# High parts of the split weights in three places of 1 MB, and the first expert's bias behind its tile's first row

## What is computed

```
u    = rms_norm(x);  proj = u @ w_in                    # 1024 x 4608
conv = silu(layer_norm(depthwise_conv31(a * sigmoid(g)))) @ w_conv_out
attn = block attention with ALiBi and q/k norm (8 heads) @ w_attn_out
h    = x + (sigmoid(gates) * [conv, attn] mixed) @ w_out
moe  : top 4 of 32 experts; each expert 1024 -> 2048 -> 1024 (clamped SwiGLU)
out  = h + sum of the chosen experts, weighted
```

## Time and profile before

| what | value |
|---|---|
| median of 3 runs | 1077.91 us (1076.74 to 1078.06) |
| the profiled execution | 1077.8 us, span of its instructions 1076.0 us |
| mean granted PE clock | 0.917 of full |
| PE busy | 901.7 us (84%) |
| DVE busy | 440.4 us (41%) |
| ACT busy | 253.9 us (24%) |
| DMA | 432.96 MB, mean 402 GB/s over the span |
| chain that ended last | PE 59%, DMA 31% |

### The profile page before, as it was taken

How to read it: one execution, slowest core, us unless ns; L and a number is a source line. 1 busy time by engine, 2 the same in 40 slices (tenths; PEclk the granted TensorE clock), 3 DMA queues, 4 the chain that set the end, 5 groups by cost and what they waited for, 6 DMA issues and landing times.

```text
span 1076.0 us, 18595 instructions
## 1 busy us (share of the span) xinstructions
PE 901.7 (84%) x6874; PEld 407.1 (38%) x6875; DVE 440.4 (41%) x1111; ACT 253.9 (24%) x410; POOL 5.5 (1%) x35
## 2 busy tenths in 40 slices
PE   8999999987665779699966999987996965997666
PEld 8889996322211223133311333322331311332122
DVE  6998885432222214244422344432442322343222
ACT  5578753211111101122211122220121201112111
POOL 2000000000000000000000000000000000000000
PEclk9999999997888789899977999997998988998788
DMA  9754699999999999999999999999999999999997
GB/s 329 281 191 142 264 385 416 421 431 428 434 434 434 431 430 429 432 432 434 435 429 430 432 431 435 434 430 430 429 435 431 434 434 430 429 432 432 434 421 290
DMA packets 34022, 432.96 MB, mean 402 GB/s; under 512 B 3029, under 2 KB 5489, under 8 KB 19152
## 3 DMA queue, kind: packets, MB, share of 16 engines
q1 hardware_dynamic: 33472, 431.99, 95.2%
q10 hardware_dynamic: 528, 0.66, 0.2%
HBM read 431.59 MB, written 1.05 MB: 402 GB/s over the span
## 4 chain that ended last, share of the span: by engine, by line
PE 59%; DMA 31%; another core or an unknown queue 5%; SPq 3%; DVE 1%; issue 0%; ACT 0%; DVEq 0%
PE bank L1564 23%; PE bank L1601 11%; PE bank L1255 9%; DMA down_even<-in_w_down 8%; DMA up_even<-in_w_up_gate 8%; DMA up_odd<-in_w_up_gate 8%; DMA down_odd<-in_w_down 6%; PE bank L1542 3%; PE bank L1495 3%; PE bank L1193 3%; PE bank L1474 3%; SPq L500 2%; SPq L504 1%; DMA down_odd<-in_w_in 1%; PE bank L1578 1%
## 5 line engine op out<-in xcount | busy, mean ns | idle before, releaser
L1564 PE MATMUL bank<-up_even,reg_r 128*32 128x512 f32 x1472 | 194.7, 685 | 77.0 <-DMA up_even<-in_w_up_gate 77.0
L1564 PE MATMUL bank<-up_odd,reg_r 128*32 128x512 f32 x1408 | 189.2, 693 | 70.0 <-DMA up_odd<-in_w_up_gate 70.0
L1149 DVE SCALAR_TENSOR_TENSOR ys<-bank,gslot,ys 64x512 fp32r<-64x512 f32 x90 | 67.4, 749 | 228.5 <-ACT ys L759 227.1
L759 ACT ACTIVATE ys<-bank,gslot 64x512 fp32r<-64x512 f32 x90 | 61.5, 683 | 315.4 <-PE bank L1601 314.3
L1564 PEld LDWEIGHTS bank<-up_even,reg_r 128*32 128x32 f32 x1472 | 51.0, 124 | 217.4 <-issue 131.8
L1564 PEld LDWEIGHTS bank<-up_odd,reg_r 128*32 128x32 f32 x1408 | 50.7, 125 | 205.1 <-issue 124.5
L753 ACT ACTIVATE reg_m<-reg_m 128x256 f32<-128x256 f32 x45 | 18.8, 418 | 428.5 <-DVE reg_m L1128 428.5
L1601 PE MATMUL bank<-down_odd,reg_r 128*32 128x512 f32 x704 | 85.1, 617 | 11.3 <-DMA down_odd<-in_w_down 11.3
L1601 PE MATMUL bank<-down_even,reg_r 128*32 128x512 f32 x736 | 83.7, 595 | 6.9 <-DMA down_even<-in_w_down 6.9
L1128 DVE TENSOR_SCALAR reg_m<-bank 128x256 f32<-128x256 f32 x45 | 19.1, 424 | 169.1 <-PE bank L1564 169.1
L753 ACT ACT_TABLE_LOAD x45 | 57.7, 1283 | 3.2 <-issue 2.5
(11 more groups left out here) (277 smaller groups left out, 1011.0 us busy)
## 6 DMA issues: line engine op xcount, KB each, us to landing
up_odd<-in_w_up_gate SPq DMA_DIRECT2D x29, 4096.0 KB, 46.5
up_even<-in_w_up_gate SPq DMA_DIRECT2D x28, 4096.0 KB, 39.7
down_even<-in_w_down SPq DMA_DIRECT2D x15, 4096.0 KB, 42.4
down_odd<-in_w_down SPq DMA_DIRECT2D x14, 4096.0 KB, 46.7
down_even<-in_w_in SPq DMA_DIRECT2D x16, 1024.0 KB, 5.2
up_even<-in_w_up_gate SPq DMA_DIRECT2D x5, 2048.0 KB, 13.7
up_odd<-in_w_up_gate SPq DMA_DIRECT2D x3, 2048.0 KB, 11.1
up_odd<-in_w_up_gate SPq DMA_DIRECT2D x6, 1024.0 KB, 45.4
```

What stands on the lines that cost most here:

```text
L759: nc.scalar.activation(ys[0:64, half, :], YB[r, :], ACT.Identity, scale=gslot[r, :]).then_inc(y_high, 1)
L1149: nc.vector.scalar_tensor_tensor(ys[64:P, half, :], YB[r, :], gslot[0:64, :], ys[0:64, half, :].bitcast(F32), ALU.mult, ALU.subtract).then ...
L1564: ins = mm(UP[q * SLOTS:(q + 1) * SLOTS, :], XT[:, k, :], up_columns(a, k, q), start=False, stop=(k == KD - 1), skip_group_check=True)
```

## The change

It has four parts.

1. **Three places for high parts.** `w_hi` becomes three tensors of 1 MB, rows 0, 1 and 2 of UP_EVEN. Half (i, b) uses place (2i + b - 2) modulo 3. A half's high part may now be written once PE is through with the half three before it: (i, 0) after (i-2, 1), and (i, 1) after (i-1, 0). Group 0's second half is kept as one piece in place 2.
2. **Row 3 of UP_EVEN is loaded early.** SP issues it behind rows 6 and 7, at about 23 us. Behind group 11 the order changes: nothing of UP_EVEN at the first half of group 11, row 0 at its second half, row 1 at the first half of group 12, row 2 at its end.
3. **Taps and low parts in a new order.** On ACT high part (2, 1) moves behind the two sigmoids of group 1. On DVE low part (2, 1) moves behind the first three tap rounds of the first two channel blocks, and later low parts are placed anew among the taps; the number of tap rounds ahead of head 0 stays 16.
4. **The first expert's bias.** The bias product ahead of the first gather goes; in its place are two products of zeros (`clear`). In the first expert's tiles row 0 clears the bank, and the bias is added behind it. In the first group PE waits for the first half of `u_hi` alone before it begins.

```diff
-        w_hi = [part("w_hi0", EVEN_AT, 0, 4096), part("w_hi1", EVEN_AT, 4096, 4096)]
+        w_hi = [part(f"w_hi{j}", EVEN_AT, 2048 * j, 2048) for j in range(3)]
...
+            return [w_hi[(2 * i + b - 2) % 3][:, :].rearrange("p (k n) -> p k n", k=4)] + [
+                t[:, 2048 * b:2048 * b + 2048].rearrange("p (k n) -> p k n", k=4) for t in (w_lo[place(i)], slots[place(i)])]
...
             load_up(0, 3, 0)
+            load_up_rows(0, 3, 4, 0)
...
             for b in range(2):
                 half_used(sp, OUT_W, b)
-                load_up_rows(0, 2 + b, 3 + b, 0)
+                if b == 1:
+                    load_up_rows(0, 0, 1, 0)
                 load_down(0, b, 1 + b, 0)
             half_used(sp, OUT_W + 1, 0)
-            load_up_rows(0, 0, 1, 0)
+            load_up_rows(0, 1, 2, 0)
             load_down(0, 2, 3, 0)
             used(sp, OUT_W + 1)
-            load_up_rows(0, 1, 2, 0)
+            load_up_rows(0, 2, 3, 0)
...
-                if 2 <= i < ATT_W:
-                    half_used(act, i - 2, b)
+                if i >= 2:
+                    half_used(act, *((i - 2, 1) if b == 0 else (i - 1, 0)))
...
-            for b in range(2):
-                weights_high(2, b)
+            weights_high(2, 0)
             for b in range(2):
                 (sigmoids of group 1)
+            weights_high(2, 1)
...
-            for b in range(2):
-                weights_low(2, b)
+            weights_low(2, 0)
...
-                taps(0, 5, (2 * b, 2 * b + 1))
+                taps(0, 3, (2 * b, 2 * b + 1))
+                if b == 0:
+                    weights_low(2, 1)
...
-            taps(5, 6); low(3,0); taps(6, 7); low(3,1); taps(7, 9); low(4,0); taps(9, 10); low(4,1); taps(10, 14); low(5,0); low(5,1)
+            low(3,0); taps(3, 5); low(3,1); taps(5, 7); low(4,0); taps(7, 9); low(4,1); taps(9, 10); low(5,0); taps(10, 11); low(5,1)
...
-            taps(14, 15); low(6,0); taps(15, 16); low(6,1)
+            taps(11, 13); low(6,0); taps(13, 15); low(6,1); taps(15, 16)
...
-            bias(0)
+            for j in range(2):
+                clear(j)
...
-                                 start=False, stop=(k == KD - 1), skip_group_check=True)
+                                 start=(first and k == 0), stop=(k == KD - 1), skip_group_check=True)
...
+                    if first and k == 0:
+                        bias(n, clear=False)
```

More of the change, by code:

```diff
@@ L299, in place @@
             return 1 + (i - 1) % 2 if i else 0
-        def w_whole(i):
-            return [t.rearrange("p (k n) -> p k n", k=KD) for t in (w_hi[i % 2][:, :], w_lo[place(i)][:, :], slots[place(i)])]
         def w_half(i, b):
-            return [t[:, 2048 * b:2048 * b + 2048].rearrange("p (k n) -> p k n", k=4)
-                    for t in (w_hi[i % 2], w_lo[place(i)], slots[place(i)])]
+            return [w_hi[(2 * i + b - 2) % 3][:, :].rearrange("p (k n) -> p k n", k=4)] + [
+                t[:, 2048 * b:2048 * b + 2048].rearrange("p (k n) -> p k n", k=4) for t in (w_lo[place(i)], slots[place(i)])]
+        first_low, first_whole = [t.rearrange("p (k n) -> p k n", k=KD) for t in (w_lo[0][:, :], slots[0])]
+        first_split = [w_hi[2][:, :].rearrange("p (k n) -> p k n", k=KD), first_low[:, :, 256:512], first_whole[:, :, 256:512]]
         def w_split(i, b):
-            if i == 0:
-                return [t[:, :, 256 * b:256 * b + 256] for t in w_whole(i)]
-            return w_half(i, b)
+            return first_split if i == 0 else w_half(i, b)
         def arrived(eng, i, b):
@@ L404, in load_parameters @@
                 sp.dma_start(wr[:], w_router.rearrange("(p k) n -> p k n", k=KD)).then_inc(small_in, 16)
-            first = w_whole(0)[2]
+            first = first_whole
             for c in range(4):
@@ L849, in _ @@
                 dve.wait_ge(a_ready, b + 1)
-                taps(0, 5, (2 * b, 2 * b + 1))
+                taps(0, 3, (2 * b, 2 * b + 1))
+                if b == 0:
+                    weights_low(2, 1)
             early_taps = 16
-            taps(5, 6)
             weights_low(3, 0)
-            taps(6, 7)
+            taps(3, 5)
             weights_low(3, 1)
+            taps(5, 7)
+            weights_low(4, 0)
             taps(7, 9)
-            weights_low(4, 0)
+            weights_low(4, 1)
             taps(9, 10)
[L860 to L863, removed]
+            weights_low(5, 0)
+            taps(10, 11)
+            weights_low(5, 1)
             dve.wait_ge(qk_std, 1)
@@ L875, in _ @@
                 nc.vector.tensor_tensor(v, v, f, ALU.mult).then_inc(qk_scaled, 1)
-            taps(14, 15)
+            taps(11, 13)
             weights_low(6, 0)
+            taps(13, 15)
+            weights_low(6, 1)
             taps(15, early_taps)
-            weights_low(6, 1)
             def attention_low(c):
@@ L1203, in product3_by_part @@
                     for k in range(n):
+                        if (a, b) == (0, 0) and k % 4 == 0:
+                            pe.wait_ge(u_hi_ready, k // 4 + 1)
                         if b == 1 and k % 4 == 0:
@@ L1209, in first_group_bank @@
             def first_group_bank(low):
-                w = w_whole(0)
+                w = first_split
                 u = group_use(0, 1)
                 pe.wait_ge(w_hi_ready, 1)
-                pe.wait_ge(u_hi_ready, 2)
                 claim(u)
                 for c in range(2):
-                    ins = product3_by_part(bank[u % 4][:, c * T:(c + 1) * T], lambda a, k: w[a][:, k, (2 + c) * P:(3 + c) * P],
+                    ins = product3_by_part(bank[u % 4][:, c * T:(c + 1) * T], lambda a, k: w[a][:, k, c * P:(c + 1) * P],
                                            lambda a, k: u_r[a][:, k, :], KD, low)
@@ L1221, in channel_group_bank @@
                 split(i, b)
-                w = w_whole(i)
+                w = [w_half(i, 0), w_half(i, 1)]
                 u = group_use(i, b)
@@ L1226, in channel_group_bank @@
                     ch = 2 * b + c
-                    ins = product3(bank[u % 4][:, c * T:(c + 1) * T], lambda a, k: w[a][:, k, ch * P:(ch + 1) * P],
+                    ins = product3(bank[u % 4][:, c * T:(c + 1) * T], lambda a, k: w[k // 4][a][:, k % 4, ch * P:(ch + 1) * P],
                                    lambda a, k: u_r[a][:, k, :], KD, before=before if c == 0 else None)
@@ L1237, in _ @@
                         pe.wait_ge(g0_in[k // 2], 16)
-                    ins = mm(bank[U_G % 4][:, c * T:(c + 1) * T], w_whole(0)[2][:, k, c * P:(c + 1) * P], xg[:, k, :],
+                    ins = mm(bank[U_G % 4][:, c * T:(c + 1) * T], first_whole[:, k, c * P:(c + 1) * P], xg[:, k, :],
                              start=(k == 0), stop=(k == KD - 1))
@@ L1491, in _, with bias @@
             mm(bank[U_WIDE % 4][0:E, 0:1], tri[0:E, 0:E], wide[:], start=True, stop=True).then_inc(bank_full[U_WIDE % 4], 1)
-            def bias(n):
+            def bias(n, clear=True):
                 pe.wait_ge(sel_ready, n + 1)
-                mm(UP[:], sel[:], bup[:], start=True, stop=False, skip_group_check=True)
+                mm(UP[:], sel[:], bup[:], start=clear, stop=False, skip_group_check=True)
             pe.wait_ge(counts_read, 1)
             pe.wait_ge(bup_in, 64)
-            bias(0)
+            for j in range(2):
+                clear(j)
             freed(pe, U_WIDE)
```

## The result

| | before | after |
|---|---|---|
| median | 1077.35 us (8 runs, 1076.52 to 1078.92) | 1081.53 us (8 runs, 1079.35 to 1084.28) |
| profiled execution, its span | 1077.8, 1076.0 | 1080.56, 1078.7 |

A forecast was written before the change was run, and what follows sets the result against it. The saturated DMA stream was taken to bound the kernel. The early MB's -2.44 us was given back by PE's release being 2.6 us late against 2.6 - 2.44 of remaining cover: 0.0, so 1077.8 us, range 1075.3 to 1080.0.

The forecast's parts named there:

- Where the stream is full: DMA at its end from the fifth slice on; by the windows busy at share 1.00, 430 GB/s, from 141 to 1056 us.
- DVE's waits: Before head 0, DVE newly idles 1.7 us for the transposes and 4.9 for high part (2,1); head 0 at 83.7, 5 us late.
- Up to 0.3 us later ... I take 0: Group 3's raw weights behind the early row: a delay up to 0.3 us would be hidden by late DVE; cost 0.
- PE held 1.9 us, then 0.7: PE waits for DVE's scores 1.9 us before scores(1) and another 0.7 before scores(2).
- s: Lateness of the releases behind groups 11 and 12 from PE being held: 1.9 + 0.7 = 2.6 us.
- The larger of -2.44 and s - 2.6: Rule for the time change: moved MB gains at most 2.44 us; 2.6 us of queued transfers cover late releases.
- the sum of the first paragraph: Time is the end of the DMA stream's last hole, plus what is still to move at 430 GB/s, plus a short tail.
- The bias: At the first gather and tile: tables and first tile start 0.7 us earlier (0 to 1.3); the release behind row 0 does not decide.
- B: Rival, groups 2 to 4: late low parts hold PE; two slips of a us give s 4.5, time 1079.7; chance 0.14.
- A: Rival: PE is held less (scores(1) below 1 us), stream nearly full, gain arrives: 1075.4 to 1076.2; chance 0.21.
- C: Rival: the early MB's move does not act; 1077.8 as well, but PE's release unmoved at 173.8; chance 0.05.
- D: Rival: an uncovered MB lands 0.7 us sooner, so cover at 173.81 is 3.3 us: time 1077.1; chance 0.08.

The follow-up runs named there:

- late MB less: Kernel before with 3 MB instead of 4 of the third expert's down weights loaded, at about 200 us: 0.9975, -2.7 us.
- later row 3: Changed kernel with row 3 of UP_EVEN issued behind group 7's weights (about 82 us) instead of at 23 us: 1.0025, +2.7 us against before.
- busy hole: Changed kernel with nine products of zeros on PE ahead of the wait of scores(1): 1.0035, +3.8 us against before.
- Twelve additions: Kernel before with twelve idle additions on DVE ahead of head 0, nothing of the change: 1.0052, +5.6 us.
- MB less early: Kernel before with row 2 of UP_EVEN for the first expert never loaded behind group 11, cleared by POOL instead: 0.9995, -0.5 us.
- mended kernels: Changed kernel with DVE's wait filled by twelve taps and row 3 behind group 7: 1.0004, +0.4 us against before; with the bias's old place too: 0.9997, -0.3.
- wait filled: Changed kernel with twelve taps of the first two channel blocks moved into DVE's 4.8 us wait, later taps dealt anew: 1.0007, +0.8 us against before.
- six additions: Kernel before with six idle additions on DVE (3.5 us) ahead of head 0: 1.0008, +0.9 us.

## Why the prediction was wrong, step by step

- **What bounds the kernel**: right. The late MB less gave 2.7 us, close to the 2.44 of the sum.
- **Where the stream is full**: it is from the sixth slice on in the earlier trace rows (the fifth has 0.6), not from the fifth. Nothing in the sum rests on it.
- **DVE's waits**: right (1.66 and 4.79 us for 1.7 and 4.9; head 0 at 84.63 for 83.7). Most of the 0.9 us missing is the next item.
- **"Up to 0.3 us later ... I take 0"** for raw half (3,0): failed. It came 1.6 us later, 0.2 of it since its issue was later. The row issued at 23.5 landed after 15.4 us, at 38.9, past the issue of group 3's weights at 35.0; my "through by about 36" overlapped with them, and I still took nothing for it. My cover for it was DVE's own lateness, which was used up: DVE waited another 0.84 us there, and PE 0.4 us for the low part. The price in the release is 1.2 us by the kernel with the early load undone, and 2.7 by the later row 3, which kept its clock as well; the raw half came as late in two traces without an early row.
- **PE held 1.9 us, then 0.7**: the first was 2.27, and PE was 0.6 us late before it. The second did not come, as PE, slowed, reached scores(2) after DVE; it came with 0.37 us in the kernels with the later row 3 and with the busy hole, whose clock was kept there. In its place came a term that the sum did not have: behind the hole PE's clock was at the lower level for part of the next us, 24 products in 4.55 instead of about 3 us. From scores(1) to scores(2) passed 8.6 us instead of 7.1, so 1.5 us; the same 8.6 stand in the two other kernels whose clock fell there. So s was 0.6 + 2.3 + 1.5 = 4.4, not 2.6.
- **"The larger of -2.44 and s - 2.6"**: this is the step that failed worst. With the measured s of 4.4 it still gives 4.4 - 2.6 = 1.8 us, where 3.9 were measured. Two errors are in it. Cover lets one release be late; it does not let the whole stream be late, since the last hole ahead of it moves by s as well, and the sum of the first paragraph (end of the last hole plus what is to be moved) already says so. Twelve additions: s 5.0, loss 5.6, with the old cover in place. And the cover itself was read from issue to landing, less an uncovered landing; but that landing time goes from 4.7 to 8.6 us over the traces, with and without the MB in the queue. By the first paragraph's sum alone, and with my own s, the change was 2.6 - 2.44 = +0.2, plus the hole that the missing MB opens. From the rows I had, that hole is at most the uncovered landing less its bytes and less what is still ahead, 5.1 - 2.44 - 0.2 = 2.5: up to 1080.5 us, without the clock's 1.5.
- **The bias**: right, nothing in the time. But the release behind row 0 is not 0.7 us sooner by it: 11.97 us behind the release of group 12 with either place of the bias, once the clock is at 1.00. The 2.08 us of the old bias in the earlier trace rows were the lower clock of that execution (1.12 at 179.76 in the kernel with a MB less early).
- **Rivals**: B named the place (low part (3,0) slipping) and the direction, but with the same cover taken off, so its 1079.7 was too low. A is refuted by the mended kernels, where PE isn't held and the full gain still doesn't come; C by the release at 178.25. D is the same rule with 0.7 us more of cover, a figure that no row and no run gives; the twelve additions refute the rule for it too.

How the releases and times go together (lateness of the release behind group 12, change of the time in us):

| kernel | MB moved or left out early | late | change |
|---|---|---|---|
| after | yes | 4.4 | +3.9 |
| early load undone | no | 3.2 | +3.7 |
| busy hole | yes | 3.0 | +3.8 |
| row 3 later | yes | 1.7 | +2.7 |
| wait filled | yes | 0.5 | +0.8 |
| filled, row 3 later | yes | -0.2 | +0.4 |
| the same, old bias | yes | 0.1 | -0.3 |
| twelve additions | no | 5.0 | +5.6 |
| six additions | no | 1.7 | +0.9 |
| a MB less, early | yes | 0.0 | -0.5 |
| bias part alone | no | -0.2 | +0.3 |

In each row "change = lateness, less 0 to 0.5 where the MB is gone" lies within the interval of the change. That is weaker than it looks. The intervals are about 1 us to either side, each lateness is from one execution, and the executions of some kernels differ by 3 to 5 us (wait filled: 1075.7 to 1081.3). The rows at 3.0, 3.2 and 4.4 us of lateness can't be told apart by their changes.

What stays open: the split of the loss between the hole and the clock was not run by itself (the run meant for it lost its gain at the first tile), and the 1.5 us for the clock is read from traces, not from a change in time. How often raw half (3,0) comes late in a kernel without the early row is open as well.

## What to carry to other kernels

When one transfer stream bounds a kernel, its time is the end of the last hole plus what is still to move: lateness ahead of that hole counts in full, however deep the queue is behind it (here 5.0 us late, 5.6 us lost). Bytes taken out of the stream are worth their time only if the queue stays filled where they were; look at the GB/s of one-us windows around the next release, not at landing times. Read a term of a few tenths of a us from more than one trace of the same kernel. And before idling is put on an engine "that is late anyway", ask what the sum of the idling does to the engine that waits for it.

## What the runs showed of the hardware

- A hole in PE ahead of scores(1) of 1.12 us (six additions) and of 1.71 us (row 3 later) left the granted clock at 1.00; holes of 2.02, 2.27 and 3.57 us were followed by 0.72, 0.60 and 0.60 at 88 to 92 us. From scores(1) to scores(2) then took 8.6 us instead of 7.1, so the clock cost 1.5 us, of the size of the hole.
- At the first tile (176 to 190 us) the granted clock was 1.00 in nine traces, 0.88 in three and 0.76 in one; the same stretch of work took 11.97 us, 12.7 to 13.0 and 14.3.
- A megabyte was worth 0.5 us (-0.5 to 1.5) left out ahead of 174 us and 2.7 us (1.6 to 3.8) left out late.
- A 1 MB DMA issued at 173.6 to 178.8 us with three others behind it landed after 4.7 to 8.6 us, with ranges that overlap for a queue with a further MB in it (6.6 to 8.6) and without (4.7 to 7.6).
